# Four key chunks of each layer's sample cache land in buffers of their own, called for with the fourth query chunk

## What is computed

```python
def mem_attend(h, k, v, w_q, w_o):
    B, T, _ = h.shape
    q = (h @ w_q).reshape(B, T, MEM_HEADS, MEM_HD)
    s = jnp.einsum('bthd,bmhd->bhtm', q, k).astype(jnp.float32) * (MEM_HD ** -0.5)
    pr = jax.nn.softmax(s, axis=-1).astype(h.dtype)
    o = jnp.einsum('bhtm,bmhd->bthd', pr, v).reshape(B, T, D_MODEL)
    return o @ w_o

def layer(i, x, conv_prev, rec_prev, mk, mv):
    ...
    x = x + y
    x = x + mem_attend(rms_norm(x, norm_mem[i]), mk, mv, mem_w_q[i], mem_w_o[i])
    ...
xs, r, c = layer(i, xs, state_lru_conv[j], state_lru_h[j], cache_mem_k[i], cache_mem_v[i])
```

## Time and profile before

| | |
|---|---|
| median of 3 runs | 1989.22 us |
| profiled execution | 1987.67 us |
| its span, first to last instruction | 1985.9 us |
| busy: TensorE matmul / weight load | 1852.8 us (93%) / 1596.0 us (80%) |
| busy: VectorE / ScalarE / GpSimd | 1466.5 us (74%) / 1244.4 us (63%) / 186.1 us (9%) |
| moved by DMA | 558.73 MB, mean 281 GB/s |
| chain that ended last | PE 80%, issue 7%, DVE 7%, DMA 3%, ACT 2%, POOL 1% |

### The profile page before, as it was taken

One profiled execution on the slowest core, in us unless ns is written; L12 is line 12 of the kernel. 1 busy time (PEld: TensorE's weight loads), 2 busy tenths in 40 slices (PEclk: granted clock), 3 DMA queues, 4 the chain that ended last, 5 costly groups with the idle time before them and its releaser, 6 DMA issues.

```text
span 1985.9 us, 31992 instructions
## 1 busy us (share of the span) xinstructions
PE 1852.8 (93%) x10920; PEld 1596.0 (80%) x10920; DVE 1466.5 (74%) x1764; ACT 1244.4 (63%) x1603; POOL 186.1 (9%) x227
## 2 busy tenths in 40 slices
PE   6998989999899997998599999999999999999994
PEld 6997869999799776887388888888888888888883
DVE  7588446663588568433499898988988889898884
ACT  6575245443475254312487888878888787877873
POOL 3021111000134510101100000000000000000001
PEclk9999989999899998998799999999999999999997
DMA  7647588754443931556399999999999999999993
GB/s 264 233 130 244 216 326 339 269 166 149 160 135 130 340 109 44 197 212 238 115 401 371 385 356 377 372 360 391 360 375 372 362 389 364 385 358 371 379 371 142
DMA packets 151104, 558.73 MB, mean 281 GB/s; under 512 B 16496, under 2 KB 16496, under 8 KB 149568
## 3 DMA queue, kind: packets, MB, share of 16 engines
q1 hardware_dynamic: 139248, 508.58, 69.2%
q10 hardware_dynamic: 6832, 28.44, 3.5%
q0 software_dynamic: 4896, 20.18, 2.7%
HBM read 520.61 MB, written 36.52 MB: 281 GB/s over the span
## 4 chain that ended last, share of the span: by engine, by line
PE 80%; issue 7%; DVE 7%; DMA 3%; ACT 2%; POOL 1%; POOLq 0%; SPq 0%; ACTq 0%; DVEq 0%
PE ps L1728 24%; PE ps L1730 24%; PE ps L1729 24%; DVE w_lo L1106 2%; PE ps L2143 1%; PE ps L2028 1%; DMA raw<-in_stream 1%; PE ps L1827 1%; PE ps L1858 1%; POOL rt L2187 1%; PE ps L1874 1%; DMA y_rows<-ye 1%; PE ps L1759 1%; ACT w_hi L700 1%; PE ps L1849 0%
## 5 line engine op out<-in xcount | busy, mean ns | idle before, releaser
L1629 DVE TENSOR_TENSOR w_lo<-raw,w_hi 128x1024 fp32r<-128x1024 f32 x672 | 786.5, 1219 | 49.4 <-ACT w_hi L1036 47.7
L1036 ACT ACTIVATE w_hi<-raw 128x1024 fp32r<-128x1024 f32 x672 | 704.5, 1060 | 139.6 <-PE ps L1730 123.7
L1728 PE MATMUL ps<-w_hi,xe_hi 128*128 128x512 f32 x896 | 358.2, 400 | 4.7 <-DVE w_lo L1629 4.7
L1730 PE MATMUL ps<-w_hi,xe_lo 128*128 128x512 f32 x896 | 354.5, 396 | 0.0
L1729 PE MATMUL ps<-w_lo,xe_hi 128*128 128x512 f32 x896 | 354.0, 395 | 0.0
L700 ACT ACTIVATE w_hi<-raw 128x1024 fp32r<-128x1024 f32 x212 | 220.5, 1050 | 166.3 <-PE ps L1730 116.8
L1106 DVE TENSOR_TENSOR w_lo<-raw,w_hi 128x1024 fp32r<-128x1024 f32 x212 | 266.3, 1269 | 69.6 <-ACT w_hi L700 69.1
L1728 PE MATMUL ps<-h_hi,w_hi 128*128 128x288 f32 x928 | 280.0, 302 | 11.2 <-DVE w_lo L1106 6.8
L1729 PE MATMUL ps<-h_lo,w_hi 128*128 128x288 f32 x928 | 275.8, 297 | 0.0
L1730 PE MATMUL ps<-h_hi,w_lo 128*128 128x288 f32 x928 | 274.9, 296 | 0.0
L1728 PEld LDWEIGHTS ps<-w_hi,xe_hi 128*128 128x128 f32 x896 | 168.9, 189 | 43.1 <-DVE w_lo L1629 5.1
(11 more groups left out here) (396 smaller groups left out, 2550.8 us busy)
## 6 DMA issues: line engine op xcount, KB each, us to landing
raw<-in_experts SPq DMA_DIRECT2D x672, 512.0 KB, 5.5
raw<-in_stream SPq DMA_DIRECT2D x261, 512.0 KB, 4.5
rest<-in_stream SPq DMA_DIRECT2D x28, 512.0 KB, 10.6
x_rows<-zeros ACTq DMA_DIRECT2D x1, 13824.0 KB, 58.9
out_ssd_s<-s_new ACTq DMA_DIRECT2D x16, 512.0 KB, 7.0
xs<-x_rows POOLq DMA_DIRECT2D x9, 512.0 KB, 4.7
y_rows<-ye POOLq DMA_DIRECT2D x9, 512.0 KB, 7.4
out_k<-kmem ACTq DMA_DIRECT2D x2, 1024.0 KB, 7.4
```

Of the source, the lines that this page charges most:

```text
L1036: act.activation(w_hi[:, (NSPLIT + p) % HL, :], raw[:, slot, :], ACT.Copy) \
L1629: dve.tensor_tensor(w_lo[:, (NSPLIT + p) % HL, :], raw[:, (NRING + p) % RAW, :], w_hi[:, (NSPLIT + p) % HL, :].bitcast(F32), ALU.subtract) \
L1728: pe.matmul(out, l_hi, r_hi, start=start, stop=False)
L1730: return pe.matmul(out, l_lo, r_hi, start=False, stop=stop)
```

## The change

The first four key chunks of each layer (two sequences) get the place "home": four buffers of 4096 bytes a partition, two in `S[10]` and two in `S[9]`, the memory of `att_lo` and `att_hi`. They leave the ring, so the ring has 8 chunks fewer in all. SP calls for them just before the layer's fourth query chunk, after a wait for the last user of that memory: in layer 0 the group of the last prompt values of layer 1 and `y_done` of 8, in layer 1 `y_done` of 12. Their landings are counted on the semaphores of the split places 7 to 10. `places()` shifts the split places behind them, so that the 14 of them start four chunks later.

```diff
+HOMES = 4
...
+    home = {a + n: n for a in starts for n in range(HOMES)}
     for a in starts:
         for n in range(2 * HL):
             o = ORDER[a] - HL + n // 2
-            free[a + RAW + n] = (o % HL + HL * (n % 2), o)
+            free[a + HOMES + RAW + n] = (o % HL + HL * (n % 2), o)
...
+        elif k in home:
+            at.append(("home", home[k]))
...
+        homes = [at(f"home{n}", [CH], F32, (S[10], S[9])[n // 2] + n % 2 * 4096) for n in range(HOMES)]
...
-            same = (("split", s), ("soon", s - RAW))
+            same = (("split", s), ("soon", s - RAW), ("home", s - RAW))
...
+            if kind == "home":
+                return homes[n][:, :]
...
+            def keys_home(l):
+                if l == 0:
+                    sp.wait_ge(full, KEY["v", 1, 1, 1] + 1)
+                    sp.wait_ge(y_done, KD)
+                else:
+                    sp.wait_ge(y_done, KD + GROUPS)
+                first = NEED[KEY["s scores", l, 0]] - 2
+                for k in range(first, first + HOMES):
+                    sp.dma_start(landing_place(k), t["stream"][k, :, :]).then_inc(landing(k)[0], 16)
+
             for i in range(NSTAT):
...
-                if kind == "soon":
+                for l in range(2):
+                    if TAKER[i] == KEY["q", l, 3]:
+                        keys_home(l)
+                if kind in ("soon", "home"):
                     continue
```

## The result

Eleven runs of each kernel on one chip: the changed kernel's median is 1979.07 us (1974.48 to 1992.03), that of the kernel before 1996.61 (1983.71 to 1999.97). The ratio is 0.9942, with a 95% interval of 0.9921 to 0.9964. The time forecast for the changed kernel, 1978, is met; but the kernel before is slower than the three runs shown had it, the gain forecast from its profile (10.8 us) is larger than what the change gives, and the interval takes in both faster by over 0.5% and within it. The times of both kernels fall in two groups some 10 us apart, and the two medians, 17.5 us apart, lie in different ones: that of the kernel before in its upper group, that of the changed kernel in its lower.

A forecast was written before the change was run, and what follows sets the result against it. Two TensorE waits on late value-chunk loads, 15 us together, were what the change could reach: 5.8 + 5.3 = 11.1, less 0.3, 10.8 us, from the median 1989.22 to 1978.4, said as 1978. Range: 1973 less 1 for spread, to 1985.

The forecast's parts named there:

- The mechanism: In both layers' attention, four early key chunks spare ring places, so the last value chunks land 4 to 5 us early.
- the next late thing: After the value products, the first "mem out" weights still wait for the tenth value chunk's ring place.
- Rival C: At the value products: values late all the same, or the wait moves elsewhere; gain 0, 1989 us; chance 0.07.
- D: Expert loop slower through shifted ring places; 1.35 us a pass eats the gain, 2.6 us gives 1999; chance 0.06.
- the base: Starting time of the kernel before: profiled execution 1987.67 us, median of the runs 1989.22, 1.55 us above it.
- The sum: "mem out" starts 5.8 us earlier in layer 0 and 5.3 in layer 1, 11.1 us, less 0.3: 10.8 us.
- lands after 3.6 us: First "mem out" weights in layer 0: a load into an empty queue lands 3.6 us after its call, at 268.5.
- The clock: TensorE's clock falls to half in the gap before "mem out" as before; counted 0, bounds 4 us gained or lost.
- A: Clock stays up in the gap before "mem out": 4 us more, 14.8 us gained in all, 1974 us; chance 0.10.
- Contention: Four early key loads delay layer 0's query chunks; cost taken as 0.3 us, bounds 0 and 5.1.
- B: Query chunks come late in layer 0 at the full price of 5.1 us: gain 6, 1983 us; chance 0.15.
- Faster by over 0.5% or within?: Whole kernel against the 0.5% (10 us) threshold: faster 0.55, within 0.40, slower 0.05.

The follow-up runs named there:

- the next eleven: The changed kernel run again with nothing edited; ratio to the kernel before 0.9973 (0.9949 to 0.9997).
- ordered six homes: Changed kernel with six key chunks in own buffers, not four, and the first two "mem out" weights halved before the sample's outputs are copied; ratio to kernel before 0.9858.
- doubled sums: TensorE makes the scan's third group of running sums twice; ratios to kernel before: on it 0.9981, on the changed kernel 0.9940 and 0.9922, with six buffers 0.9872.
- called together: Kernel before, with the load of the first of the last four value chunks called some 0.86 us later, close to the other three; ratio to kernel before 0.9999.
- the second: Profile of the kernel before run again with nothing edited; ratio 0.9984 (0.9964 to 1.0004), profiled span 1991.0 us.
- calling late: Changed kernel with its four key chunks called for behind the query chunks, not with the fourth query chunk; ratio to kernel before 0.9947.

## Why the prediction was right and wrong

**The mechanism held.** No value product waits, the last value chunk lands at 263.27 where 262.7 was read from the earlier trace rows, and the next late thing is the first "mem out" weights, called for when the tenth value chunk closes (264.65). Rival C is out. So is D: a pass of the expert loop takes 121.3 us as before.

**The step that failed first is the base**: "the profiled execution took 1987.67 us ... the median of the runs, 1989.22, lies 1.55 us above it". Both are of the lower group, in which only 45 of 107 runs of this kernel lie; the median of all is 1994.6. The three runs shown spanned 11.2 us, 1987.37 to 1998.58, as much as the whole forecast, and the prediction took their middle as the kernel's time without asking what the 11 us were. The time of 1978 is right for the lower group of the changed kernel (1978.1), half of whose runs lie in the other, at 1985.1 to 1992.0: all of them above the 1985 at which the prediction's range ends. That the first eleven runs have their median at 1979.07 is luck: 8 of them are of the lower group, 3 of the next eleven are, and the median of all 22 is 1983.3.

**The sum was too large by a quarter.** Forecast 5.8 + 5.3 = 11.1 us, less 0.3. Measured, with means over the profiles above (layer 0: four without homes there, five of the change; layer 1: three and six): 17.04 - 12.48 = 4.6 us and 16.71 - 11.40 = 5.3. Layer 1 is as forecast. In layer 0 the step "lands after 3.6 us" failed: the load landed 4.2 to 4.8 us after its call in the five profiles, 4.4 on average, and 3.5 to 3.8 in layer 1. That is 0.8 of the 1.2 us that layer 0 lacks; the other 0.4 is that the first profile's 17.43 lies above the mean of 17.04. The view of DMA queues from the call to the landing shows a packet of another queue in layer 0,

```profile
q1 hardware_dynamic: 338, 1.27, 76.0%
q8 instruction: 1, 0.02, 1.8%
```

and none of it in layer 1:

```profile
q1 hardware_dynamic: 187, 0.70, 76.8%
```

The same holds in all five. That this packet costs the 0.8 us was not tried, and one row speaks against it: in layer 1 of the kernel before, the load called for at 902.03 has such a packet beside it as well and lands after 3.69 us. So why it landed late in layer 0 stays open. By the Trainium skill ("DMA: Bandwidth & Descriptors", "Anatomy of one DMA") the load would be an estimated 3.2 us; the shortest of these loads took 3.46.

**The clock was counted 0 and cost about 0.9 us.** It fell in both gaps, as forecast, and A did not happen. But "mem out" now starts nearer to the fall: 1.5 us behind it in layer 0, where it was 9.2. In layer 0 half speed lasted to 282.24 before, 4.4 us into "mem out", and lasts to 278.36 now, 5.4 us into it; in layer 1 it is 4.7 and 6.2 us. The price that the prediction read from the earlier trace rows, 1 - 17/33 of that time, makes 0.5 + 0.7 us in this pair; the means of the table, over the same profiles as above, show 28.10 - 27.63 = 0.5 and 41.01 - 40.62 = 0.4 (the change's six lie from 39.6 to 42.0). So 9.9 - 0.9 = 9.0 us, beside 8.3 and 8.5 between the groups. A's price was right: the kernel with the ordered six homes kept the clock, and behind the gaps it is 27.63 - 25.70 = 1.9 and 40.62 - 38.47 = 2.2 us shorter than the kernel before, where A said 4.

The other two stretches in which the first pair of profiles differs are at least in part scatter. Without the doubled sums, the scan takes 57.8 us in both lower-group profiles of the kernel before (called together in one of them), and 57.8, 59.1 and 60.8 with the change; in the last two the granted clock was 0.50 for 3.4 and 6.8 us towards its end. Whether that is the change's stays open. From the experts' last product to the end it is 27.9 us in the first profile, the shortest of all 14, 28.9 in the second, and 28.4 to 29.2 with the change.

**Contention was counted 0.3 and cost nothing.** The fourth query chunk lands 6 us later, yet from the first query product to the first key product it is 35.9 us in both profiles, and calling late changed nothing. The transfers did take time from one another: the prompt's values to memory, called for on ScalarE's queue, land 10.7 us after their call where it was 7.0. That agrees with the Trainium skill, by which transfers of different engines run on the same 16 DMA engines and interleave ("DMA: Bandwidth & Descriptors", "Issuing engines are not separate DMA queues"). B is wrong because nobody waited for the later landings; that ScalarE's idle time and the late use of the chunk hide them is the prediction's account, and no run tried it apart.

**Faster by over 0.5% or within?** 0.55 and 0.40 were given. The first 11 runs say 0.58%, all of them, group against group, 8.4 us or 0.42%: within, by a little. The 2.4 us by which the sum was too large decide that; of these 1.2 are layer 0's, 0.9 the clock's, less the 0.3 of contention, and 0.6 stay within what these means scatter. The 0.58% of the first 11 runs is the larger figure because more of the changed kernel's runs were of the lower group (8 of 11) than of the kernel's before (4 of 11).

## What to carry to other kernels

When the runs of a kernel spread by as much as the gain that is forecast, find out from the granted clock by stage whether they are one group or two before choosing the base; one profiled execution belongs to one of them. When a late load is removed, the next late load sets the gain: here it was the first weights behind it, and giving two more chunks a place and halving those weights early was worth more than the change itself. If TensorE's stand becomes short enough that its clock does not fall (in "mem out" here 1.00 us kept it at 1.00, where 3.1 to 4.8 us did not), the engine gives more than the wait; and when limits of an order come from a resource, moving that resource frees work that should have stayed behind.

## What the runs showed of the hardware that was not expected

- The same program spends about 58 or about 70 us in the same scan, with its granted clock at 1.00 or at 0.50 for some 24 us of it, and the course differs from run to run.
- A 512 KB load called for 0.86 us behind another on SP's idle queue landed 1.3 to 3.5 us behind it, in 26 places of 13 profiles: in the same code of the kernel before 3.5 and 3.0 us in one profile, 2.5 and 1.5 in the next. Loads called for 0.4 to 0.5 us behind others landed mostly 1.2 to 1.3 us behind.
- Calls that began 0.86 us later landed no later at the end of their group: 12.2 us after the first value product, where three profiles with the earlier call have 11.6 to 12.5, and 11.4 where they have 11.9 to 12.4.
- Stands of 0.58 and 1.00 us of TensorE left the granted clock at 1.00 in "mem out"; the stands of the changed kernel, 4.79 us in layer 0 and 3.11 in layer 1, did not. In the scan, waits of 1.06 to 2.87 us came before a fall to 0.50.
